# Turning the latents in the score banks, and copying the first gates' sums earlier, in the second block of a two-block transformer

## What is computed

```
xn = rms_norm(h, norm_mix_pre)
proj = xn @ w_in                      # 1024 x 5120
qkv_a = proj[..., :2304]              # 12 heads of dilated attention, 64 wide
q_c = proj[..., 2304:2816]            # latent of the queries, 512 wide
kv_c = proj[..., 2816:3072]           # latent of keys and values, 256 wide
k_pe = proj[..., 3072:3104]
gates = sigmoid(proj[..., 3104:] + b_gate)        # 2048 wide
o_a = mixer_dilated(qkv_a, pos) @ w_o_a
q  = (rms_norm(q_c, q_norm) @ w_uq) ...           # 8 heads
kv = (rms_norm(kv_c, kv_norm) @ w_ukv) ...
o_b = attention(q, k, v) @ w_o_b
mix = (g_a * o_a + g_b * o_b) @ w_out
```

## Time and profile before

| | |
|---|---|
| runs shown | 1999.50, 2001.23, 2003.59 us; median 2001.23 |
| profiled execution | 1996.97 us |
| its span in the profile | 1995.1 us |
| mean granted clock of TensorE over the span | 0.919 |
| TensorE busy | 89% of the span |
| VectorE busy | 63% |
| ScalarE busy | 41% |
| GpSimd busy | 7% |
| DMA | 332.54 MB, mean 167 GB/s |

### The profile page before, as it was taken

The page is one execution under the profiler, slowest core; times in us unless marked ns, Lnnn a source line. Parts: engine busy times, 40 slices in busy tenths (PEclk is TensorE's granted clock), DMA queues, the critical chain, the costliest instruction groups (busy, mean ns, idle before and its releaser), DMA issues. The chain is left out here.

```text
span 1995.1 us, 21568 instructions
## 1 busy us (share of the span) xinstructions
PE 1780.7 (89%) x8718; PEld 1483.6 (74%) x8718; DVE 1249.9 (63%) x1705; ACT 826.5 (41%) x999; POOL 134.2 (7%) x120
## 2 busy tenths in 40 slices
PE   4997998899889998859768999999997899788998
PEld 2775777887678876749657888888876866678987
DVE  5455784468545544554636898888896555566643
ACT  5322332422112225222324677767654433445542
POOL 1220001100110011220010000000020000000000
PEclk8897998999999999875777999999998999898999
DMA  7422342355445433210044888888874521134553
GB/s 284 107 106 84 106 154 79 112 184 201 174 163 211 150 110 127 85 53 11 1 147 154 321 325 324 334 321 322 326 261 147 190 85 53 64 127 161 188 190 126
DMA packets 61433, 332.54 MB, mean 167 GB/s; under 512 B 16835, under 2 KB 17410, under 8 KB 28177
## 3 DMA queue, kind: packets, MB, share of 16 engines
q1 hardware_dynamic: 56080, 321.54, 44.9%
q10 hardware_dynamic: 4354, 6.32, 0.9%
q0 software_dynamic: 896, 3.26, 0.5%
HBM read 329.96 MB, written 1.13 MB: 166 GB/s over the span
## 5 line engine op out<-in xcount | busy, mean ns | idle before, releaser
L1922 DVE TENSOR_TENSOR wlo__65<-raw__64,whi__66 128x2048 fp32r<-128x2048 f32 (+2 forms) x68 | 156.9, 2308 | 120.9 <-ACT whi__66 L1415 120.9
L1415 ACT ACTIVATE whi__66<-raw__64 128x2048 fp32r<-128x2048 f32 (+2 forms) x68 | 127.1, 1869 | 141.5 <-DMA raw__64<-in_ffn_w 48.7
L1922 DVE TENSOR_TENSOR wlo__61<-raw__60,whi__62 128x2048 fp32r<-128x2048 f32 (+3 forms) x56 | 125.3, 2238 | 87.5 <-ACT whi__62 L1415 87.5
L1922 DVE TENSOR_TENSOR wlo__69<-raw__68,whi__70 128x2048 fp32r<-128x2048 f32 (+4 forms) x52 | 110.1, 2117 | 44.9 <-ACT whi__70 L1415 44.9
L1415 ACT ACTIVATE whi__62<-raw__60 128x2048 fp32r<-128x2048 f32 (+3 forms) x56 | 102.9, 1838 | 76.8 <-DMA raw__60<-in_ev_w_in 22.5
L1415 ACT ACTIVATE whi__70<-raw__68 128x2048 fp32r<-128x2048 f32 (+4 forms) x52 | 90.5, 1741 | 37.5 <-DMA raw__68<-in_od_w_out 16.1
L1955 DVE SCALAR_TENSOR_TENSOR wsum__71<-raw__68,silu_rows 128x1024 f32<-128x1024 f32 x84 | 99.9, 1220 | 3.1 <-DMA raw__68<-in_ada_w 2.6
L2876 POOL TENSOR_TENSOR keep__58<-keep__58,keep__59 128x1 f32<-128x1 f32 (+3 forms) x48 | 49.2, 1027 | 715.6 <-DVE keep__58 L1994 715.6
L2177 DVE TENSOR_REDUCE keep__58<-ps 128x1 f32<-128x256 f32 (+1 forms) x104 | 56.5, 544 | 28.1 <-PE ps L880 21.3
L1415 ACT ACTIVATE whi__139<-raw__137 128x2048 fp32r<-128x2048 f32 (+2 forms) x15 | 26.2, 1744 | 110.3 <-DMA raw__137<-in_ffn_w 110.3
L1922 DVE TENSOR_TENSOR wlo__138<-raw__137,whi__139 128x2048 fp32r<-128x2048 f32 (+2 forms) x15 | 31.2, 2079 | 56.6 <-ACT whi__139 L1415 56.6
(11 more groups left out here) (1100 smaller groups left out, 5387.8 us busy)
## 6 DMA issues: line engine op xcount, KB each, us to landing
raw__68<-in_ada_w SPq DMA_DIRECT2D x26, 1024.0 KB, 5.0
raw__64<-in_moe_w SPq DMA_DIRECT2D x24, 1024.0 KB, 6.6
raw__60<-in_moe_w SPq DMA_DIRECT2D x24, 1024.0 KB, 6.6
raw__68<-in_moe_w SPq DMA_DIRECT2D x16, 1024.0 KB, 5.9
raw__220<-in_moe_w SPq DMA_DIRECT2D x16, 1024.0 KB, 5.1
raw__224<-in_moe_w SPq DMA_DIRECT2D x16, 1024.0 KB, 6.2
raw__60<-in_ada_w SPq DMA_DIRECT2D x15, 1024.0 KB, 6.4
raw__64<-in_ffn_w SPq DMA_DIRECT2D x13, 1024.0 KB, 4.9
```

What stands on the lines that cost most here:

```text
L1415: e.activation(t.hi(), t.raw(), ACT.Copy).then_inc(*did("hi", i))
L1922: e.tensor_tensor(t.lo(), t.raw(), t.hi().bitcast(F32), ALU.subtract).then_inc(*did("lo", i))
```

## The change

The constant `GATE_AT` of gate 0 goes from 0 to -2, so that its copy belongs to step -1. ScalarE calls `gated(-1)` ahead of the small latents' upper halves: the two copies of gate 0, and the feed that goes with them, stand there and no longer in step 1 of the attention. On TensorE the four turns of the latents take their banks from ring x in place of ring 8.

```diff
@@ constants of the attentions
-    GATE_AT = {(n, t): HEADS["a2"].filled.index(16 * n + 12 + 4 * t) if n else 0 for n in range(4) for t in range(2)}
+    GATE_AT = {(n, t): HEADS["a2"].filled.index(16 * n + 12 + 4 * t) if n else -2 for n in range(4) for t in range(2)}
@@ tensor_program
             proj(("lat", g), x4(AT2s), 2, KT, w_in[:, c0:c0 + w_], w_, rdy("s"))
             if g:
                 for t in range(2):
-                    head_turn(("lat", 0, t), XRs[(8 + t) % 3], 4, [("latn", 0, t)])
+                    head_turn(("lat", 0, t), XRs[(8 + t) % 3], 4, [("latn", 0, t)], "x")
         fill = gates(x4(AT2s), w_in)
         advance(fill, 16)
         for t in range(2):
-            head_turn(("lat", 1, t), XRs[(10 + t) % 3], 2, [("latn", 1, t)])
+            head_turn(("lat", 1, t), XRs[(10 + t) % 3], 2, [("latn", 1, t)], "x")
         attend("a2", fill)
@@ scalar_program
-        for t in range(2):
-            lat_hi(1, t)
-
         def gated(i):
             for n_ in range(4):
                 for t in range(2):
...
                         e.activation(GA[t][:, n_ * 512:(n_ + 1) * 512], bank("gate", n_, t),
                                      ACT.Copy).then_inc(*did("gcopy", n_, t))
                         empties(("gate", n_, t), ("gcopy", n_, t))
+        gated(-1)
+        for t in range(2):
+            lat_hi(1, t)
         attend("a2", gated)
```

## The result

The changed kernel takes 1988.97 us (median of 6 runs, 1987.38 to 1993.29) against 2001.16 us before (6 runs). The medians differ by 12.2 us. The ratio of the runs' means is 0.9943, 95% interval 0.9929 to 0.9957, so 11.4 us less, between 8.6 and 14.2. The forecast was 1989.8, or 11.4 us less. Its profiled execution took 1989.28 us with a span of 1987.5.

A forecast was written before the change was run, and what follows sets the result against it. TensorE, busy 1780.7 of 1995.1 us, was taken as the bound. Stalls of 7.31 + 6.12 = 13.43 us gained, 2.1 given back, make 11.4 us off the 2001.23 us median: 1989.8 us, range 1984.5 to 1996.5.

The forecast's parts named there:

- First stall: TensorE before gate 0, waiting for VectorE's scaling of the large latents: 5.44 us idle plus 1.87 us slow clock, 7.31 us.
- Second stall: TensorE between score 0 and gate 1, waiting for ScalarE's gate 0 copies: 6.12 us, with half clock.
- What is late next: At score 4: a new wait of some 2.1 us for exponential 1, score 4 starting 11.4 us earlier.
- The possible waits for L2699 at scores 1 and 2: Waits for the small latents' scaling or bank 3 before these scores: hidden, by 0.6 us at least.
- The clock: Behind score 4: the forecast gave back only the 2.1 us wait and no slow clock.
- rival (c): The score 4 wait brings slow clock, 1.2 to 1.9 us per stretch: gain 7.6 to 10.2 us, 1991 to 1994; 9%.
- A sign that I had named for being wrong: Half-clock stretches appearing between scores 4 and 23 would show the prediction wrong; no size given.
- The parts alone: Either edit by itself: 6.3 us gained by the rings alone, 5.1 us by the copies alone.
- Rival (d): Through the whole attention the clock swings and the kernel gets slower, 2020 us at worst; 3%.

The follow-up runs named there:

- e3: Changed kernel, but VectorE makes the second gate 1 tile's lower half in step 1, no longer ahead of the small latents' scaling; 1985.68 us, ratio 0.9928.
- e4: Changed kernel, but the tile converted between exponentials 0 and 1 is converted in step 3 of the attention; 1987.36 us, ratio 0.9939.
- e5: Changed kernel, but TensorE does the first mla_w_uq product before turning the attention's merged result, in banks 4 and 5; 1986.89 us, ratio 0.9924.
- e6: Changed kernel with the edits of e3 and e5 together; 1983.43 us, ratio 0.9897.
- e9: The kernel before, unchanged, run again for a second profile; 1997.83 us (one run).
- e10: Changed kernel, but four more steps of the gates are filled in from step 3 of the dilated attention; 1997.37 us, ratio 0.9982.
- e11: Kernel of e6, but two more steps of the gates are filled in from step 3 of the dilated attention; 1993.08 us, ratio 0.9966.
- e2: Kernel before, with only ScalarE's two gate 0 copies moved ahead of the small latents' upper halves; 1992.29 us, ratio 0.9969.
- e1: Kernel before, with only the four turns of the latents moved to ring x; 1994.78 us, ratio 0.9985.
- e8: The rings-only kernel of e1 run again for a second profile, against the kernel before; 1996.81 us, ratio 0.9974.

## Why the prediction was right, and where it was not

- **First stall, 7.31 us**: score 0 came 21.39 - 13.76 = 7.63 us nearer, 0.3 more than forecast. Gate 0's tiles were ready.
- **Second stall, 6.12 us**: from score 0 to score 1 it takes 1607.44 - 1605.23 = 2.21 us in place of 8.33, exact.
- **What is late next**: a wait of "some 2.1 us" at score 4, and score 4 "11.4 us earlier". Measured 2.37 and 11.45. The cause was named rightly: e3 and e4 each took away one link of the chain (the lower half ahead of the small latents, the conversion between exponentials 0 and 1), and the wait fell to 1.05 us and to nothing.
- **The possible waits for L2699 at scores 1 and 2** didn't show, as forecast.
- **The clock** is the step that failed. I gave rival (c) 9% and counted the clock as kept behind a wait of 2.1 us. Both profiles of the changed kernel, and that of e5, which has the same wait, have 6.8 us of half clock there, worth 3.1 us and not the 1.2 to 1.9 us that one stretch was priced at. That price was read behind the two stalls of before. Half clock lasted 6.8 us there too, but it began inside the wait, and TensorE worked through only some 4.1 and 3.2 us of it; behind score 4 it works through all 6.8. A sign that I had named for being wrong, half clock between scores 4 and 23, is there as well: the stretch from 1618.3 to 1625.1.
- **It was made good by something that I had not counted**: around the 4.1 us wait for L2151 the half clock lasted 6.8 us before and 3.4 us in both profiles of the changed kernel, and so did a second stretch just ahead of the second attention. Score 4 to the first score of the second attention took 137.85 - 36.72 = 101.1 us before and 127.90 - 25.27 = 102.6 after, so of the 3.1 us lost 1.6 came back. By the profiles the end is 9.7 us nearer, which is a gain of rival (c)'s range (7.6 to 10.2) and not the forecast's; the timed 11.4 us has an interval of 8.6 to 14.2 and covers both. That the median hit the forecast within 1 us is in part luck. The second profile of the kernel before has these two stretches at 3.4 us as well, and 6.8 us at another place, at the same end (406.2). So that they are shorter isn't shown to be the change's doing.
- **The parts alone**: 5.1 for the copies held (4.5 in the profile, 6.2 timed, interval 3.6 to 8.8). 6.3 for the rings didn't: the wait was longer as forecast, but the longer wait and the half clock behind it took nearly all. By the profiles the two edits are worth more together (9.7 us) than apart (4.5 and nothing), because the second one keeps the wait from arising that the first one lengthens; the times, with their intervals of some 3 us each way, don't settle it.
- **Rival (d)**, the swinging clock through the whole attention, didn't come. The Trainium skill's rule (TensorE: Matmul & The Clock Gate, section "A second HAM failure mode: psum-queue depth-cycling") spoke of short idle times that make the clock swing. For the swing through the whole attention this trace disagrees: from 1625.3 to 1693.0 there are two waits of 0.81 us and the clock is 1.00 throughout. What the changed kernel does have is one stretch of half clock behind one wait of 2.4 us, and e3, e6 and e9 have one behind a wait of 0.80 us.

## What to carry to other kernels

When a stall is removed, follow the engine that released it on its own timeline: it moves only as far as its own queue lets it, and the next wait can be worked out to some tenths of a microsecond from the old trace. Price each wait that is left, or made, with its clock: 1.3 us less of idle time was worth 3.7 us at the end here, as a wait of 1.05 us kept the clock and one of 2.4 us lost it. That is what these profiles have: in the dilated attention half clock came behind each of the six waits of 2.35 to 2.69 us (changed kernel twice, e5, e10 twice, e11), and behind none of the five of 1.05 to 1.74 us (e2, e3, e4, e6, e11). It is no safe limit, since behind the shorter wait of 0.80 us it came in three profiles of eleven. And before work is moved into a wait, look at what else is keyed to that work's place, here the order in which tiles are converted.

## What the runs showed that I had not expected

- Half clock can begin well behind the wait and outlast gapless work: in the changed kernel TensorE worked for 1.6 us at full clock after its wait, and then had 0.50 for 6.8 us while it was busy all the time.
- How long it lasts depends on more than the wait. Behind waits before the same matmul of gate 1, the kernel before (4.80 us) had full clock again after 3.2 us of work, and e1 and e8 (6.24 and 6.04 us) after about 16.4 us. In the two profiles each of the changed kernel and of the rings-only kernel such stretches lie at the same place within 0.5 us, so it isn't chance alone; in the two of the kernel before one stretch appears in only one of them, and two differ in length. What decides it isn't settled.
